# Expert rows written to a table ordered by choice and token, and a final stage inside the experts' block: one change to a hybrid decoder trunk

## What is computed

```
g_idx = argmax(g_logits);  top_v, top_i = top_k(e_logits[g_idx], 2)
combine = one_hot(g_idx) x one_hot(top_i) * softmax(top_v) * g_prob[g_idx]
h_e = silu(x @ w_gate[e]) * (x @ w_up[e])           # 16 experts, 1024 -> 128
y = sum_e (h_e * combine_e) @ w_down[e]             # 128 -> 1024
h = h + y;  out = h * rsqrt(mean(h*h) + eps) * final_norm_g
```

## Time and profile before

| | us |
|---|---|
| median of 3 runs (3106.88 to 3109.52) | 3107.2 |
| the profiled execution | 3106.81 |
| its span, first to last instruction | 3105.0 |

### The profile page before, as it was taken

One profiled execution on the slowest core, in us unless ns is written; L12 is line 12 of the kernel. 1 busy time (PEld: TensorE's weight loads), 2 busy tenths in 40 slices (PEclk: granted clock), 3 DMA queues, 4 the chain that ended last, 5 costly groups with the idle time before them and its releaser, 6 DMA issues. The chain is left out here.

```text
span 3105.0 us, 41130 instructions
## 1 busy us (share of the span) xinstructions
PE 2792.4 (90%) x14110; PEld 1913.3 (62%) x14111; DVE 1688.7 (54%) x3394; ACT 1104.3 (36%) x2274; POOL 1028.0 (33%) x982
## 2 busy tenths in 40 slices
PE   8989999999976799999999899999899999579980
PEld 4668888888864465665545566666444455456760
DVE  6675556655547566666666578887222222422227
ACT  0012222222235355555555456666211122123322
POOL 1266777866613402112130201100222333011116
PEclk9999999999987699999999999999999999689995
DMA  3333234232353101110020111100864244365848
GB/s 130 132 130 109 102 109 165 101 109 102 109 183 147 36 8 59 37 65 11 30 77 20 48 55 42 42 1 1 333 192 115 93 156 137 124 237 203 351 164 316
DMA packets 150215, 355.30 MB, mean 114 GB/s; under 512 B 13840, under 2 KB 61584, under 8 KB 143888
## 3 DMA queue, kind: packets, MB, share of 16 engines
q1 hardware_dynamic: 129776, 278.47, 25.8%
q0 software_dynamic: 13824, 50.34, 4.8%
q10 hardware_dynamic: 6432, 24.12, 2.0%
HBM read 230.52 MB, written 122.36 MB: 114 GB/s over the span
## 5 line engine op out<-in xcount | busy, mean ns | idle before, releaser
L566 ACT ACTIVATE p_kept<-p_a 128x256 f32<-128x256 f32 x336 | 129.0, 384 | 463.6 <-PE p_a L512 463.5
L1536 DVE CUSTOM_DVE_ANT_0 b_prob_s<-b_pq,b_sel 128x640 f32<-128x640 f32 (+5 forms) x192 | 168.6, 911 | 129.8 <-PE b_pq L1428 123.1
L1464 PE MATMUL b_po<-b_probT,vsw 128*64 128x256 f32 (+1 forms) x1824 | 231.7, 372 | 0.0
L1389 POOL TENSOR_TENSOR b_rate<-gates,b_total 128x256 f32<-128x256 f32 x64 | 37.9, 614 | 578.5 <-DVE b_total L1550 578.5
L1831 DVE CUSTOM_DVE_ANT_0 d_prob<-d_pq,d_bias 128x1024 f32<-128x1024 f32 (+6 forms) x192 | 168.1, 910 | 68.6 <-PE d_pq L1723 66.4
L1488 ACT ACTIVATE b_prob_s<-b_prob_s,b_neg 128x1152 f32<-128x1152 f32 (+15 forms) x128 | 152.8, 1196 | 128.2 <-DVE b_neg L1544 128.0
L1428 PE MATMUL b_pq<-ks,b_q 64*128 64x512 f32 (+3 forms) x688 | 165.1, 543 | 17.0 <-DVE b_seg_max L1536 8.6
L1559 DVE COPY b_probT<-b_pt 128x512 f32<-128x512 f32 (+1 forms) x253 | 152.5, 630 | 46.3 <-PE b_pt L1451 46.0
L1723 PE MATMUL d_pq<-d_keys,d_q 64*128 64x512 f32 (+3 forms) x576 | 165.8, 561 | 4.9 <-DVE d_seg_max L1831 3.9
L1451 PE MATMUL b_pt<-ident,b_prob_s 128*128 128x128 f32 x1088 | 158.2, 282 | 7.5 <-DVE b_probT L1559 7.1
L1464 PEld LDWEIGHTS b_po<-b_probT,vsw 128*64 128x64 f32 x1824 | 107.3, 136 | 92.1 <-issue 54.3
(11 more groups left out here) (379 smaller groups left out, 6069.8 us busy)
## 6 DMA issues: line engine op xcount, KB each, us to landing
projT<-p_result SPq DMA_DIRECT2D x64, 512.0 KB, 2.8
y<-e_y ACTq DMA_DIRECT2D x43, 512.0 KB, 4.4
p_w<-in_wt SPq DMA_DIRECT2D x16, 1024.0 KB, 7.1
p_w_more<-in_wt SPq DMA_DIRECT2D x16, 1024.0 KB, 6.2
gates_T<-projT SPq DMA_DIRECT2D x64, 256.0 KB, 4.3
wgu<-in_w_gu SPq DMA_DIRECT2D x4, 4096.0 KB, 14.8
y<-b_q POOLq DMA_DIRECT2D x20, 512.0 KB, 21.2
p_xin<-in_x SPq DMA_DIRECT2D x16, 512.0 KB, 3.9
```

The costliest lines, as they stand in the source:

```text
L1464: mm = nc.tensor.matmul(po[u % 2][g * HD:(g + 1) * HD, o:o + w], s.vsw[:, kb, v0 + g * HD:v0 + (g + 1) * HD], probT[:, f % 4, g * w:(g + 1 ...
L1536: nc.vector.tensor_tensor_reduce(out=to, in0=pq[g][:, 0:nb * P], in1=away, scale=slopes[PAIRS * g + i], scalar=-3e38, op0=ALU.add, op1=ALU ...
```

## The change

The table `y` gets one row for each choice and token: 2 x 2048 rows, and behind them 6784 spare rows for what belongs to no token. The experts' results are scattered there row by row. So the two results of a tile of tokens stand in two plain pieces of 512 KB, and the last stage needs no gather.

- The zeros of the merging block go (POOL's memset and its 20 stores).
- `tokens` becomes a constant with a number for each choice and token, from 1 to 4096. From the same product DVE works out `s.index` in three instructions instead of one, and `s.row` (where each row of a tile is to be written; empty rows go to a spare row of their own). `s.slot` goes.
- ACT's 43 stores of `y[b]` go; POOL issues 43 indirect DMAs in their place (`spread_rows`): wait for the last scatter of this buffer, copy a column of `s.row` to `to[b]`, wait for both halves of `y[b]`, scatter.
- Ahead of its loop POOL clears `y[0]` and `y[1]` and scatters both to spare rows; the second waits for the first to land, and both stand before POOL's first gather in this block.
- In the loop the next gather stands ahead of the scatter.
- `finish` becomes a part of `experts`: no barrier and no new block between them. SP loads the two pieces of each tile when POOL reports that the last scatters have landed (`all_spread`), ACT stores the results, and POOL keeps the root.

```
 merge_branches, POOL:
-            nc.gpsimd.memset(zeros, 0.0).then_inc(zeroed, 1)
-            pool.wait_ge(zeroed, 1)
-            for n in range(2 * NT, MAXT):
-                nc.gpsimd.dma_start(y_t[n], zeros).then_inc(y_cleared, 16)
...
 choose_experts, DVE:
-            nc.vector.tensor_copy(s.index[:], pm[:, 0, :]).then_inc(index_copied, 1)
+            link(nc.vector.tensor_scalar(second_row[:], pm[:, 0, :], T + 0.5, -float(T), ALU.is_gt, ALU.mult))
+            link(nc.vector.scalar_tensor_tensor(out=second_row[:], in0=second_row[:], scalar=-1.0, in1=pm[:, 0, :], op0=ALU.add, op1=ALU.add))
+            nc.vector.tensor_scalar(s.index[:], second_row[:], 0.0, None, ALU.max).then_inc(index_copied, 1)
             nc.vector.tensor_copy(s.weight[:], pm[:, 1, :])
-            link(nc.vector.tensor_scalar(slot[:], slot[:], float(P), None, ALU.add))
-            link(nc.vector.tensor_copy(s.slot[:], slot[:]))
+            link(nc.vector.tensor_scalar(empty[:], pm[:, 0, :], 0.0, None, ALU.is_equal))
...
+            nc.vector.tensor_copy(s.row[:, 1:MAXT + 1], empty[:])
+            nc.vector.tensor_scalar(s.row[:, 0:1], tokens[:, 0:1], 2.0 * T + NSLOT - 1.0, None, ALU.add)
...
 experts, SP:
+            sp.dma_start(gain[:], d["final_row"]).then_inc(gain_in, 16)
+            y_t = d["y"][0:2 * T].rearrange("(k n p) c -> k n p c", k=2, p=P)
+            sp.wait_ge(all_spread, 1)
+            for t in range(NT):
+                if t >= NB:
+                    sp.wait_ge(added, t - NB + 1)
+                for k in range(2):
+                    sp.dma_start(rows[:, t % NB, k, :], y_t[k][t]).then_inc(rows_in[t % NB], 16)
...
 experts, POOL:
+            def spread_rows(i, b):
+                pool.wait_ge(spread[b], 16 * i + 16)
+                pool.sem_inc(step, 1)
+                nc.gpsimd.tensor_copy(to[b][:], s.row[:, bass.ds(2 * i + b, 1)]).then_inc(row_ready, 1)
+                pool.wait_ge(row_ready, 2 * i + b + 1)
+                pool.sem_inc(step, 1)
+                pool.wait_ge(y_copied, 4 * i + 2 * b + 4)
+                pool.sem_inc(step, 1)
+                nc.gpsimd.indirect_dma_start(d["y"], bass.IndirectOffsetOnAxis(ap=to[b][:], axis=0), y[b][:], None).then_inc(spread[b], 16)
+            for b in range(2):
+                nc.gpsimd.memset(y[b][:], 0.0).then_inc(blank, 1)
+                nc.gpsimd.tensor_copy(to[b][:], s.row[:, b * MAXT:b * MAXT + 1]).then_inc(blank, 1)
+                pool.wait_ge(blank, 2 * b + 2)
+                if b == 1:
+                    pool.wait_ge(spread[0], 16)
+                nc.gpsimd.indirect_dma_start(d["y"], bass.IndirectOffsetOnAxis(ap=to[b][:], axis=0), y[b][:], None).then_inc(spread[b], 16)
+            pool.wait_ge(x_turned, 1)
+            fetch(nc, pool, d, s, 0, s.index[:, 2:3], 3)
+            spread_rows(0, 0)
+            with pool.Fori(1, ends[NG]) as i:
+                pool.wait_ge(x_turned, 2 * i)
+                fetch(nc, pool, d, s, 1, s.index[:, bass.ds(2 * i + 1, 1)], 2 * i + 2)
+                spread_rows(i - 1, 1)
+                pool.wait_ge(x_turned, 2 * i + 1)
+                fetch(nc, pool, d, s, 0, s.index[:, bass.ds(2 * i + 2, 1)], 2 * i + 3)
+                spread_rows(i, 0)
...
+            spread_rows(ends[NG] - 1, 1)
+            spread_rows(ends[NG], 0)
+            for b in range(2):
+                pool.wait_ge(spread[b], 16 * ends[NG] + 32 - 16 * b)
+            pool.sem_inc(all_spread, 1)
...
 experts, ACT (the square of a tile, then the store of the tile two before):
-                act.wait_ge(y_copied, 4 * i + 2 * b + 4)
-                act.dma_start(y_t[2 * i + b], y[b][:]).then_inc(y_stored[b], 16)
+            def store_out(t):
+                act.wait_ge(done, t + 1)
+                act.dma_start(out_t[t], s.h[:, t, :]).then_inc(out_stored, 16)
```

More of the change, by code:

```diff
@@ L2391, in choose_experts @@
         weight = sb("weight", [P, NT, 2])
+        second_row, spare, empty = (sb(n, [P, MAXT]) for n in ("second_row", "spare", "empty"))
         pc = ctx.enter_context(nc.psum_tensor("r_pc", [P, NT, NX], fp32))
@@ L2566, in _, with experts @@
             nc.vector.tensor_copy(s.down[:, 1:MAXT + 1], expert[:])
-def experts(nc, d, s):
+def experts(nc, d, s, out):
     import concourse.bass as bass
@@ L2591, in experts @@
         py = [ctx.enter_context(nc.psum_tensor(f"e_py{k}", [P, 512], fp32)) for k in range(2)]
+        NB = 4
+        gain, stat = sb("gain", [P, D]), sb("stat", [P, NT, 4])
+        square = y[0]
+        rows = s.wgu[0][:].rearrange("p (n k c) -> p n k c", n=NB, k=2)
+        rows_in = [nc.alloc_semaphore(f"f_rows_in{b}") for b in range(NB)]
+        gain_in, all_spread, paired, added, ss_ready, var_ready, rstd_ready, done, out_stored = (nc.alloc_semaphore("f_" + n) for n in (
+            "gain_in", "all_spread", "paired", "added", "ss_ready", "var_ready", "rstd_ready", "done", "out_stored"))
+        out_t = out[0].rearrange("(n p) c -> n p c", p=P)
         gathered = s.gathered
-        y_stored = [nc.alloc_semaphore(f"e_y_stored{b}") for b in range(2)]
-        h_in, x_turned, xT_ready, gu_ready, silu_done, hid_ready, hid_turned, hidT_ready, y_ready, y_copied, \
+        to = [sb(f"to{b}", [P, 1], i32) for b in range(2)]
+        spread = [nc.alloc_semaphore(f"e_spread{b}") for b in range(2)]
+        h_in, blank, row_ready, x_turned, xT_ready, gu_ready, silu_done, hid_ready, hid_turned, hidT_ready, y_ready, y_copied, \
             group_done, cleared, step = (nc.alloc_semaphore("e_" + n) for n in (
-                "h_in", "x_turned", "xT_ready", "gu_ready", "silu_done", "hid_ready", "hid_turned", "hidT_ready",
+                "h_in", "blank", "row_ready", "x_turned", "xT_ready", "gu_ready", "silu_done", "hid_ready", "hid_turned", "hidT_ready",
                 "y_ready", "y_copied", "group_done", "cleared", "step"))
-        y_t = d["y"].rearrange("(n p) c -> n p c", p=P)
         block = ctx.enter_context(nc.Block())
@@ new lines, in _ @@
+            pool.wait_ge(gathered[0], 16 * ends[NG] + 16)
+            pool.sem_inc(step, 1)
+            spread_rows(ends[NG] - 1, 1)
+            spread_rows(ends[NG], 0)
+            for b in range(2):
+                pool.wait_ge(spread[b], 16 * ends[NG] + 32 - 16 * b)
+                pool.sem_inc(step, 1)
+            pool.sem_inc(all_spread, 1)
+            for t in range(NT):
+                pool.wait_ge(var_ready, t + 1)
+                nc.gpsimd.tensor_tensor(stat[:, t, 2:3], stat[:, t, 1:2], s.half[:, 0:1], ALU.pow).then_inc(rstd_ready, 1)
@@ L2693, in _ @@
             store(ends[NG], 0)
[L2694 to L2697, removed]
+            def store_out(t):
+                act.wait_ge(done, t + 1)
+                act.dma_start(out_t[t], s.h[:, t, :]).then_inc(out_stored, 16)
+            for t in range(NT):
+                act.wait_ge(added, t + 1)
+                if t >= 1:
+                    act.wait_ge(ss_ready, t)
+                nc.scalar.activation(square[:], s.h[:, t, :], ACT.Square, accum_out=stat[:, t, 0:1]).then_inc(ss_ready, 1)
+                if t >= 2:
+                    store_out(t - 2)
+            for t in range(NT - 2, NT):
+                store_out(t)
+            act.wait_ge(out_stored, 16 * NT)
         @block.vector
@@ L2729, in _ @@
             copy_y(ends[NG], 0)
[L2732 to L2788, removed]
@@ L2796, in normalize @@
             def normalize(t):
                 dve.wait_ge(rstd_ready, t + 1)
-                nc.vector.scalar_tensor_tensor(out=h[:, t, :], in0=h[:, t, :], scalar=stat[:, t, 2:3], in1=gain[:],
+                nc.vector.scalar_tensor_tensor(out=s.h[:, t, :], in0=s.h[:, t, :], scalar=stat[:, t, 2:3], in1=gain[:],
                                                op0=ALU.mult, op1=ALU.mult).then_inc(done, 1)
+            dve.wait_ge(h_in, 16 * 4)
             dve.wait_ge(gain_in, 16)
@@ L2938, in program @@
         s.index = sb(ctx, "index", [P, MAXT], mybir.dt.int32)
+        s.row = sb(ctx, "row", [P, MAXT + 1], mybir.dt.int32)
         s.weight = sb(ctx, "weight", [P, MAXT])
@@ L2951, in program @@
         s.h = sb(ctx, "h_again", [P, NT, D])
-        experts(nc, d, s)
-        finish(nc, d, s, out)
+        experts(nc, d, s, out)
 def lay_out(inputs):
```

43 lines of the change are left out of this document (19 added, 24 removed).

## The result

The changed kernel takes **3116.67 us** (median of 9 runs, 3112.76 to 3121.57) against 3106.88 (median of 9, 3101.57 to 3111.03): a ratio of 1.0032, 95% interval 1.0022 to 1.0043. It is slower by 0.3%, with an interval that leaves out no change, and it lies above the range that was given. The profiled execution took 3119.14 us, its span 3117.3.

| stretch | before | after | difference |
|---|---|---|---|
| up to the first transposes of the experts | 2729.42 | 2733.07 | +3.7 |
| first to last transposes (43 of them) | 282.4 | 303.5 | **+21.1** |
| last transposes to the last copy of `y` | 6.9 | 7.0 | +0.1 |
| last copy to DVE's first addition | 10.7 | 9.3 | -1.4 |
| first addition to DVE's end | 72.5 | 59.1 | **-13.4** |

What follows compares the result with a forecast made beforehand. TensorE was taken to bound the experts, and DVE waiting for gathers to stretch finishing. Terms 0.5 + 8.4 + 1.3 - 1.1 - 0.9 - 11.2 = -3.0 gave 3104 us for the median, range 3096 to 3114.

Steps and rivals of the forecast that it cites:

- Zeros, 0: Merging: dropping the memset and 20 stores gains 0, since TensorE is busy there and waits for nothing.
- choosing the experts, +0.5: Index computation: two more dependent DVE instructions start POOL's gathers later, +0.5 us; the `s.row` instructions hide under POOL's drain.
- Start, +8.4 and +1.3: Start of the experts: first gather queues behind two blank scatters beside the weights, +8.4 us; slower clock after idling, +1.3.
- the lower bound, for which +6 was given: Start of the experts: the delay if the first blank scatter lands after 4.3 us; +12 if at 15.5.
- the clock's +1.3: Start of the experts: TensorE at a lower clock after 11 us idle, 0 to 2.4 us more, middle taken.
- The loop, "0, and -1.1 in two places": Experts' loop: POOL has 1.5 us to spare per tile, so 0; gathers beside group-end weight loads gain 1.1 us.
- Hand-over, -0.9: From the experts' last copy to DVE's first addition: DVE starts at 3028.5 instead of 3029.43, -0.9 us.
- Finishing, -11.2: Last stage: loads four tiles ahead let DVE's own pace rule, 61.4 us in place of 72.5.
- the 2 us for transfers: Finishing: 2 us added because DVE will wait a little for the DMA engines near the end.
- POOL did not become the bound: Rival on the loop: scatter and gather issues stretch to 1.98 us, 6.6 us a tile, 3122 us; chance 0.09.
- Transfers did not bind the last stage: Rival on finishing: 25.2 MB at 358 GB/s take 70 us, gain only 3, kernel at 3112; chance 0.08.
- The signs that the prediction gave for being right: Third tile 7 to 12 us later, loop tile 6.16, first addition within ten, finishing tiles about 3.7, 390 GB/s or more.

Runs made afterwards that it cites:

- runs 3 and 7: 3: kernel before, gathers issued late by a wait for copies and a clear, 3126.93 us; 7: kernel before, weight loads in 4 KB packets, 3093.74 us.
- run 1: The changed kernel with each scatter one tile further back in POOL's stream, so gathers go first; 3105.23 us, ratio 0.9994.
- run 4: The changed kernel with each scatter one tile further back and without the two blank scatters; 3097.25 us, ratio 0.9962.
- run 8: The changed kernel with scatters one tile back, no blank scatters and POOL's last two roots left out; 3094.0 us, ratio 0.9954.

## Why the prediction was wrong

- *Zeros, 0, and choosing the experts, +0.5.* From the start of merging to the first transposes it takes 528.6 us on average in the three profiles that have the old code in both places (the kernel before, runs 3 and 7) and 529.2 in the eight that have the new: +0.5 as forecast, but single ones scatter by 1, so it is no more than agreement within the scatter. The other 2.8 of the +3.7 arise ahead of merging, where nothing was changed: its start lies between 2196.7 and 2205.6 in the profiles of this study, with the old code as well (2199.95, 2204.8, 2205.5).
- *Start, +8.4 and +1.3.* The third tile came 7.0 us later than the shift, the tile after it lost nothing to the clock (7.64 us in place of 7.89). The first blank scatter had landed 4.5 us after its issue, not 12: the lower bound, for which +6 was given. The two transfers behind it, beside the weights, took 13.2 and 17.7 us. (By the earlier trace rows eight packets on each engine take 6 x 8 x 16 / 50 = 15.4 us, not 12.) Where gathers come first the blanks cost 8.0 us (runs 1 and 4), so the cause was right and the clock's +1.3 did not come; beside the late gathers the blanks cost 2.6.
- *The loop, "0, and -1.1 in two places".* **This is the step that failed.** It says: "POOL's gather is issued from 2757.84 to 2758.81; the scatter's column, its gap and its issue add [...], to 2761.3", and "So POOL has 1.5 us to spare in each tile". That adds the scatter behind a gather which keeps its place. The text of the program has the gather ahead of the scatter, but of another tile: `spread_rows(i - 1, 1)` waits for 4i + 2 copies, and the last two of these are made after transposes 2i; the gather behind it needs only those transposes. So each gather stands behind copies which end 2.8 us after its own release, and behind the scatter's issue. POOL indeed had time to spare, 2.98 us in each tile; it spent it in the wrong place. In the tiles beside the last weights this cost +13.9 us, beside the group's weights before +0.9, for a forecast of -1.1. Beside the large packets no gain came with the gathers first either: the same tiles lost 2.9 us in run 1 and 2.5 in run 4.
- *Hand-over, -0.9:* -1.4 and +0.1. *Finishing, -11.2:* (72.5 - 61.4 is 11.1.) DVE's own pace as forecast, without the 2 us for transfers, -13.4; against it +2.3 behind DVE's end, where the text said "What follows the last addition stays" and POOL's drain became the last. Together -12.4 for -12.1.
- *The rivals.* POOL did not become the bound; its scatters took 980 ns on average over 41. The Trainium skill (SBUF — State Buffer, "SBUF: two separate sides") keeps GpSimd from writing descriptors while DVE runs an instruction that takes both read ports. No scatter took longer than 1.01 us, so nothing of it shows here. That does not speak against the rule: DVE's instructions in this loop all read a result of TensorE, and whether any is of that kind was not tried. Transfers did not bind the last stage: DVE was busy for 54.16 of 55 us, at 388 GB/s. The Trainium skill (DMA: Bandwidth & Descriptors, "Where 436 GB/s comes from") gives 358 GB/s as what binds; the row is above it. A slower kernel by late gathers in the loop was not among the rivals.

The signs that the prediction gave for being right nearly all came: the third tile 10.6 us later, 6.16 us a tile, DVE's first addition 9.3 us behind the last copy, 3.65 us a tile in finishing, 388 GB/s for "390 or more". None of them looks at the tiles beside the last weights, where the time went.

The loop that the prediction described, the scatter behind its gather, is that of run 1. It took 3105.2 us where 3104 was forecast, in part by luck: in its profile the first tiles cost 8.1 us for a forecast of 9.7 and the loop +2.9 for -1.1, and the last stage's faster pace was paid back by the drain.

## What to carry to other kernels

When a new instruction with a wait goes into a stream, don't ask whether the stream has time to spare, ask what its wait holds back: put the counts of the semaphores side by side and find for each request behind it the event that releases it alone. A profile with slack everywhere shows nothing of a request's lateness until other traffic comes. And a small urgent transfer that shared engines with a large one went at the pace of the large one's packets here: cutting the large loads to 4 KB rows made all four kernels in which it was tried faster, by 13 to 26 us (3106.7 to 3093.7, 3116.7 to 3102.6, 3097.25 to 3079.7, 3105.2 to 3079.4).

## What the runs showed of the hardware

- Two queues took turns nearly packet for packet at both sizes tried: 64 to 50 packets in 6 us with 32 KB against 4 KB, 367 to 306 with 4 KB each.
- POOL's drain at the end of a block took 3.5 us behind 32 gathers and the 16 roots in the kernel before, but 7.9 behind 86 scatters and gathers and the same roots. It starts with POOL's last instruction, so in run 8, where POOL was through early, it was hidden. What sets its length was not tried.
- Loads of 16 partitions with 32 KB rows were far slower than one of 128 partitions: 4.19 MB in 38 us, against 2.10 MB in 6 us.
- Two executions of the same code can stand 9 us apart before the stage in question begins (start of merging, 2196.7 to 2205.6): stretches have to be compared from an event of their own.
